# Seven-product feed-forwards: a third output bank, S4 in SBUF, additions to y ahead of the next S2 chain, slots in order of use, from the third group on

## What is computed

```
def swiglu(h, w_in, w_out):
    g, u = jnp.split(h @ w_in, 2, axis=-1)
    return (jax.nn.silu(g) * u) @ w_out
```

## Time and profile before

| | us |
|---|---|
| median of 3 runs | 3055.93 |
| lowest, highest | 3053.72, 3056.25 |
| profiled execution, its own time | 3053.14 |
| its span, first to last instruction | 3051.4 |
| TensorE busy in it | 2763.3 (91%) |
| VectorE busy | 1832.1 (60%) |
| GpSimd busy | 1509.9 (49%) |
| ScalarE busy | 1257.7 (41%) |
| mean granted clock of TensorE | 0.964 |

### The profile page before, as it was taken

One profiled execution on the slowest core, in us unless ns is written; L12 is line 12 of the kernel. 1 busy time (PEld: TensorE's weight loads), 2 busy tenths in 40 slices (PEclk: granted clock), 3 DMA queues, 4 the chain that ended last, 5 costly groups with the idle time before them and its releaser, 6 DMA issues. The chain is left out here.

```text
span 3051.4 us, 45625 instructions
## 1 busy us (share of the span) xinstructions
PE 2763.3 (91%) x17672; PEld 2453.7 (80%) x17672; DVE 1832.1 (60%) x3055; ACT 1257.7 (41%) x2315; POOL 1509.9 (49%) x982
## 2 busy tenths in 40 slices
PE   8989999999999999787889778889989999788888
PEld 6778888889998998677778677778877788677787
DVE  5787766776767784764566655565554423644444
ACT  3276432324453673333333333333455733333332
POOL 1333544445564333655664565565424444565563
PEclk7999999999999999898999899999999999999999
DMA  5324554435754222233343233343323222122221
GB/s 231 98 45 163 196 197 154 158 124 174 256 203 136 50 50 104 101 126 111 119 138 111 90 127 129 124 138 111 113 60 105 83 98 82 56 84 75 78 90 63
DMA packets 103923, 362.47 MB, mean 119 GB/s; under 512 B 12449, under 2 KB 14625, under 8 KB 102305
## 3 DMA queue, kind: packets, MB, share of 16 engines
q1 hardware_dynamic: 103714, 359.63, 35.1%
HBM read 338.61 MB, written 2.10 MB: 112 GB/s over the span
## 5 line engine op out<-in xcount | busy, mean ns | idle before, releaser
L333 POOL TENSOR_TENSOR w_lo<-raw,w_hi 128x1024 fp32r<-128x1024 f32 x259 | 655.9, 2538 | 680.7 <-ACT w_hi L327 623.3
L1159 POOL TENSOR_TENSOR w_lo<-raw,w_hi 128x512 fp32r<-128x512 f32 x261 | 347.7, 1336 | 301.2 <-ACT w_hi L1143 297.9
L327 ACT ACTIVATE w_hi<-raw 128x1024 fp32r<-128x1024 f32 x267 | 279.1, 1055 | 429.6 <-PE ps L356 387.2
L356 PE MATMUL ps<-ffn_hi,w_hi 128*128 128x512 f32 (+1 forms) x844 | 320.2, 379 | 136.9 <-DVE y L1452 92.9
L356 PE MATMUL ps<-h_hi,w_hi 128*128 128x512 f32 (+1 forms) x1096 | 363.2, 346 | 9.1 <-DVE h_lo L632 4.4
L356 PE MATMUL ps<-h_lo,w_hi 128*128 128x512 f32 (+1 forms) x1096 | 357.2, 341 | 0.0
L356 PE MATMUL ps<-h_hi,w_lo 128*128 128x512 f32 (+1 forms) x1096 | 357.1, 341 | 0.0
L356 PE MATMUL ps<-n_hi,w_hi 128*128 128x256 f32 (+1 forms) x880 | 304.8, 346 | 18.5 <-DVE n_lo L890 9.5
L356 PE MATMUL ps<-ffn_lo,w_hi 128*128 128x512 f32 (+1 forms) x844 | 313.2, 371 | 0.0
L356 PE MATMUL ps<-ffn_hi,w_lo 128*128 128x512 f32 (+1 forms) x844 | 311.9, 369 | 0.0
L356 PEld LDWEIGHTS ps<-ffn_hi,w_hi 128*128 128x128 f32 x844 | 167.3, 198 | 179.5 <-DVE y L1452 109.9
(11 more groups left out here) (393 smaller groups left out, 7369.7 us busy)
## 6 DMA issues: line engine op xcount, KB each, us to landing
raw<-w_stream SPq DMA_DIRECT2D x441, 512.0 KB, 3.4
modraw<-mod_stream SPq DMA_DIRECT2D x102, 512.0 KB, 5.2
mod_extra<-mod_stream SPq DMA_DIRECT2D x74, 512.0 KB, 5.3
mod_pair<-mod_first SPq DMA_DIRECT2D x7, 1024.0 KB, 12.5
l_qs<-l_q_hi SPq DMA_DIRECT2D x32, 128.0 KB, 2.3
l_qs<-l_q_lo SPq DMA_DIRECT2D x32, 128.0 KB, 2.3
l_qs<-l_q_hi SPq DMA_DIRECT2D x16, 192.0 KB, 2.9
l_qs<-l_q_lo SPq DMA_DIRECT2D x16, 192.0 KB, 3.5
```

The source lines that it names most:

```text
L327: nc.scalar.activation(w_hi[:, c % RING, :], raw[:, c % RING, :], ACT.Copy).then_inc(hi_ready, 1)
L333: nc.gpsimd.tensor_tensor(w_lo[:, c % RING, :], raw[:, c % RING, :], w_hi[:, c % RING, :].bitcast(F32), ALU.subtract).then_inc(lo_ready, 1)
L356: mm = nc.tensor.matmul(out, w[a], x[b][:, off:off + n], start=first and i == 0, stop=last and i == 2)
L1159: ins = nc.gpsimd.tensor_tensor(lo, item_raw(c, k), hi.bitcast(F32), ALU.subtract)
```

## The change

The last line of `ffn` gives all three feed-forwards banks 5, 6 and 2 for outputs, so that output n waits for the addition of output n-3. Bank 2 no longer holds S2; both chunks form S2 in bank 7, and S4 goes to a new SBUF buffer, `down_last`. The low parts of both S4 move from VectorE to GpSimd. The items take their slots, and GpSimd its low parts, in the order in which TensorE uses them, with outputs among them. Seven-product groups are groups 2 to 9; group 1 becomes direct. On VectorE the additions 0 to 2 stand ahead of S2 of the next group, addition 3 ahead of its low part and S4, addition 4 ahead of the second half of `seven_hidden` (now split off as `seven_third` and `seven_hidden`), S2 of b=1 moves to the start of the next group, `pair_u` goes ahead of bS2's low part, and mods part 1 goes from the end of the group to before addition 0. TensorE no longer starts outputs 0 and 1 with chunk 2g alone before it waits for chunk 2g+1. In group 0 both parts of the mods go ahead of the second hidden product and the input sums go behind the additions; their copies and low parts move to group 1. The core of the diff:

```
-                    outs=(5, 6, 2) if name == "l0_ffn" else (5, 6))
+                    outs=(5, 6) if name == "l0_ffnc" else (5, 6, 2))
...
-    POOL_LOWS = [A11, S3, S1, A12, A22] + [PARTS + k for k in (A11, S3, S1, A12, A22)] + [OUT_Q, OUT_Q + 1, OUT_Q + 2]
-    DVE_LOWS = [S2, S4, PARTS + S2, PARTS + S4]
+    POOL_LOWS = [A11, S3, S1, A12, PARTS + A11, A22, S4, PARTS + S3, PARTS + S1, PARTS + A12, OUT_Q, OUT_Q + 1, PARTS + A22,
+                 PARTS + S4, OUT_Q + 2]
+    DVE_LOWS = [S2, PARTS + S2]
...
-    SEVEN = NG - 2
+    SLOT_ORDER = PE_ORDER[:12] + [OUT_Q, OUT_Q + 1] + PE_ORDER[12:] + [OUT_Q + 2, OUT_Q + 3]
+    HI_ORDER = [A11, S2, S3, S1, A12, PARTS + A11, A22, S4, PARTS + S2, PARTS + S3, PARTS + S1, PARTS + A12, OUT_Q, OUT_Q + 1,
+                PARTS + A22, PARTS + S4, OUT_Q + 2, OUT_Q + 3]
+    FIRST_SEVEN, LAST_SEVEN = 2, NG - 2
+    SEVEN = LAST_SEVEN - FIRST_SEVEN + 1
...
     def turn_of(g, k):
 
-        return ITEMS * (g - 1) + k + min(max(g - 2, 0), 4)
+        i = SLOT_ORDER.index(k) if k < ITEMS else ITEMS
+        return 2 + ITEMS * (g - FIRST_SEVEN) + i + min(g - FIRST_SEVEN, 4)
...
-        for n in range(2):
-            bank_free(n)
-            out_part(n, 0)
         pe.wait_ge(hid_ready, CREDIT + f["m"] + 2 * g + 2)
-        for n in range(2):
-            out_part(n, 1).then_inc(out_ready, 1)
-        for n in range(2, 4):
+        for n in range(4):
             bank_free(n)
             out_part(n, 0)
             out_part(n, 1).then_inc(out_ready, 1)
...
     def seven_s4(dve, f, c, g, b):
-        dve.wait_ge(q_low_dve, before_items(f, g, 4) + 2 * b + 1)
-        y = down_bank(b)
-        nc.vector.tensor_tensor(y, raw_quarter(c + 2 * b, A12), y, ALU.subtract).then_inc(down_chain, 1)
+        i = chunks_done(f, g, b)
+        dve.wait_ge(q_low_dve, before_items(f, g, 2) + b + 1)
+        if i >= 1:
+            low_there(dve, f, c, g if b else g - 1, S4 if b else PARTS + S4)
+        nc.vector.tensor_tensor(down_last[:], raw_quarter(c + 2 * b, A12), down_bank(), ALU.subtract).then_inc(down_chain, 1)
...
+        seven_s2(dve, f, c, g, 1)
+        seven_u(dve, f, g, 0)
         item_low_dve(dve, f, c, g, PARTS + S2)
         seven_s4(dve, f, c, g, 1)
-        seven_u(dve, f, g, 0)
         seven_c22(dve, f, g, 0)
-        item_low_dve(dve, f, c, g, PARTS + S4)
         mods(0)
         seven_u(dve, f, g, 1)
+        seven_third(dve, f, g, 0)
         seven_hidden(dve, f, g, 0)
         ffn_hidden_lo(dve, f, 2 * g + 1, 0)
         seven_c22(dve, f, g, 1)
-        if g < SEVEN:
+        mods(1)
+        dve.wait_ge(out_free, f["free0"] + CREDIT + 8 * g)
+        for n in range(3):
+            add(n)
+        if g < LAST_SEVEN:
             seven_s2(dve, f, c + 6, g + 1, 0)
+        add(3)
+        if g < LAST_SEVEN:
             item_low_dve(dve, f, c + 6, g + 1, S2)
             seven_s4(dve, f, c + 6, g + 1, 0)
-        dve.wait_ge(out_free, f["free0"] + CREDIT + 8 * g)
-        for n in range(4):
-            add(n)
+        seven_third(dve, f, g, 1)
+        add(4)
         seven_hidden(dve, f, g, 1)
-        if g < SEVEN:
-            seven_s2(dve, f, c + 6, g + 1, 1)
-            item_low_dve(dve, f, c + 6, g + 1, S4)
-        for n in range(4, KC):
+        for n in range(5, KC):
             add(n)
         ffn_hidden_lo(dve, f, 2 * g + 2, 0)
-        mods(1)
...
         full_pool(pool, f, h, 0)
+        split_lo(pool, c0 + 4)
         full_pool(pool, f, h, 1)
-        split_lo(pool, c0 + 4)
+        split_lo(pool, c0 + 5)
+        split_lo(pool, c0 + 6)
         full_pool(pool, f, h, 2)
+        split_lo(pool, c0 + 7)
         full_pool(pool, f, h, 3)
...
+            if f["index"] > 0 and g == 0:
+                mods(g, 1, group)
             ffn_mult(dve, f, 2 * g + 2, 2 * gd, c + 2, d)
...
+            if f["index"] > 0 and g == 0:
+                in_sums_dve(dve, f)
+                return
             mods(g, 1, group)
```

More of the change, by code:

```diff
@@ L1065, in item_at @@
     def item_at(turn):
-        for g in range(1, SEVEN + 1):
-            if turn_of(g, 0) <= turn < turn_of(g, 0) + ITEMS:
-                return g, turn - turn_of(g, 0)
+        for g in range(FIRST_SEVEN, LAST_SEVEN + 1):
+            i = turn - turn_of(g, SLOT_ORDER[0])
+            if 0 <= i < ITEMS:
+                return g, SLOT_ORDER[i]
     def slot_views(f, turn):
@@ L1366, in seven_act @@
     def seven_act(act, f, c, g):
+        more = g < LAST_SEVEN
         def ahead(k):
[L1369 removed]
+            if more:
                 item_hi(act, f, c + 6, g + 1, k)
[L1372 to L1373 removed]
+        down_copy(act, f, g, 1)
         seven_first_copy(act, f, g, 0)
[L1375 removed]
+        for k in (PARTS + S2, PARTS + S3, PARTS + S1, PARTS + A12, OUT_Q, OUT_Q + 1):
             item_hi(act, f, c, g, k)
         seven_silu_first(act, f, g, 0)
[L1378 removed]
+        item_hi(act, f, c, g, PARTS + A22)
+        item_hi(act, f, c, g, PARTS + S4)
         seven_first_copy(act, f, g, 1)
[L1380 removed]
+        item_hi(act, f, c, g, OUT_Q + 2)
+        item_hi(act, f, c, g, OUT_Q + 3)
         seven_silu_second(act, f, g, 0)
[L1382 removed]
         ffn_hidden_hi(act, f, 2 * g + 1, 0, c, 0)
[L1384 to L1385 removed]
+        if more:
             ahead(A11)
@@ L1391, in seven_act @@
             prepare_last_act(act, f, c, 0)
+        seven_silu_first(act, f, g, 1)
+        if more:
+            ahead(A12)
+            ahead(PARTS + A11)
+        else:
             prepare_last_act(act, f, c, 1)
-        seven_silu_first(act, f, g, 1)
-        if g < SEVEN:
-            down_copy(act, f, g + 1, 1)
-            ahead(A12)
+        seven_silu_second(act, f, g, 1)
+        if more:
             ahead(A22)
+            ahead(S4)
         else:
             prepare_last_act(act, f, c, 2)
-        seven_silu_second(act, f, g, 1)
-        if g < SEVEN:
-            ahead(S4)
-            ahead(PARTS + A11)
         ffn_hidden_hi(act, f, 2 * g + 2, 0, c + 6, 0)
-        if g == SEVEN:
+        if not more:
             prepare_last_act(act, f, c, 3)
@@ L1506, in ffn_pool @@
         full_pool(pool, f, h, 0)
+        split_lo(pool, c0 + 4)
         full_pool(pool, f, h, 1)
-        split_lo(pool, c0 + 4)
+        split_lo(pool, c0 + 5)
+        split_lo(pool, c0 + 6)
         full_pool(pool, f, h, 2)
+        split_lo(pool, c0 + 7)
         full_pool(pool, f, h, 3)
-        for i in range(5, 8):
+        for i in range(8, 2 + 6 * FIRST_SEVEN):
             split_lo(pool, c0 + i)
-        for g in range(1, SEVEN + 1):
-            seven_pool(pool, f, c0 + 2 + 6 * g, g)
+        for g in range(FIRST_SEVEN, LAST_SEVEN + 1):
+            c = c0 + 2 + 6 * g
+            down_pool(pool, f, c, g, 0)
+            for k in (A11, S3, S1, A12, PARTS + A11):
+                item_low_pool(pool, f, c, g, k)
+            down_pool(pool, f, c, g, 1)
+            for k in POOL_LOWS[5:]:
+                item_low_pool(pool, f, c, g, k)
+            item_low_pool(pool, f, c, g, ITEMS - 1)
         for i in range(FFN_BLOCKS - RING, FFN_BLOCKS):
@@ L1848, in step @@
                 split_lo_dve(dve, c + 4)
+            if f["index"] > 0 and g == FIRST_SEVEN - 1:
+                mods(g, 0, group)
             ffn_mult(dve, f, 2 * g + 1, 2 * gd, c, d)
@@ L1852, in step @@
                 split_lo_dve(dve, c + 5)
-            if f["index"] > 0:
-                in_sums_dve(dve, f)
-            mods(g, 0, group)
-            if f["index"] > 0:
+            last_direct = f["index"] > 0 and g == FIRST_SEVEN - 1
+            if last_direct:
                 in_sums_low(dve, f)
-                seven_s2(dve, f, c + 6, 1, 0)
+                seven_s2(dve, f, c + 6, g + 1, 0)
+            else:
+                mods(g, 0, group)
+            if f["index"] > 0 and g == 0:
+                mods(g, 1, group)
             ffn_mult(dve, f, 2 * g + 2, 2 * gd, c + 2, d)
-            if f["index"] > 0:
-                item_low_dve(dve, f, c + 6, 1, S2)
-                seven_s4(dve, f, c + 6, 1, 0)
             if f["held"]:
```

102 lines of the change are left out of this document (43 added, 59 removed).

## The result

| | before | changed |
|---|---|---|
| median, us | 3054.82 | 2860.85 (4 runs, 2858.45 to 2864.26) |
| ratio to before, 95% interval | | 0.9366 [0.9349, 0.9382] |
| profiled execution, its own time; its span | 3053.14; 3051.4 | 2862.70; 2860.5 |
| GpSimd busy in it | 1509.9 (49%) | 1570.1 (55%) |
| mean granted clock | 0.964 | 0.981 |

The change takes 6.3% off the time: 194 us by the medians, 190.4 between the two profiled executions. The forecast was 2870. Where the time came from, by the stretches (columns as in the earlier trace rows: length, busy PE, PEld, DVE, ACT, POOL, PEclk, DMA, GB/s), in this order: groups 0 and 1 of F1, F2, F3; groups 2 to 9 of F1, F2, F3; one group of F1, one of F2, one of F3.

What follows compares the result with a forecast made beforehand. VectorE's order and the two output banks were taken to bind, not the work. Gains of 54.1, 11.3, 53.3 and 67.1 sum to 185.8 us off 3053.1: 2867.3, plus 2.8 for the median, 2870; range 2820 to 2930.

Steps and rivals of the forecast that it cites:

- Groups 0 and 1: First two groups of each feed-forward: group 0 from 122.7 to 68.6 us, group 1 from 118.1 to 106.8, in all three.
- Third bank and additions ahead, F3: Groups 2 to 9 of the third feed-forward: no output waits, 31.8 us a group, gain 53.3 us.
- Mods of part 1 before addition 0: Groups 2 to 9, first two feed-forwards: mod blocks land late, output n=3 waits 3.5 us; 36.5 us a group.
- The clock: Groups 2 to 9, first two feed-forwards: lower granted clock costs 1.3 us a group, bounds 0 and 3.5.
- The earlier slots from group 7 on: First two feed-forwards: slots come one item earlier from group 7, 35.2 us a group where earlier ones take 36.5.
- Group 2: First two feed-forwards: group 1's part 1 mods still stand ahead of group 2's pair_u, 2.5 us each, 5.0 together.
- GpSimd: Seven-product groups: GpSimd takes 25.8 us a group in the third feed-forward, 28 to 30 in the first two.
- Joining the halves of n=0 and n=1: Outputs 0 and 1: costs nothing while hidden chunk 2g+1 is there, 0.87 us of cover; without cover 1.4 us.
- the mod blocks in time: Rival, first two feed-forwards: only VectorE's own 5.3 us count, 33.6 us a group, total 2831; chance 0.20.
- The clock's rival: Rival, first two feed-forwards: blocks land at T+22, clock loses today's 8%, +2.5 us in 16 groups, 2910; chance 0.20.
- GpSimd as the bound: Rival, seven-product groups: 20 items at 2.25 us make 45 us a group, slower at 3114; chance 0.06.
- The bank does not help: Rival: additions wait behind something else on VectorE, groups 2 to 9 stay unchanged, total 2990; chance 0.04.

Runs made afterwards that it cites:

- experiment 1: Changed kernel with the third output bank undone for the seven-product feed-forwards (banks 5 and 6 only): 2912.0 us, ratio 0.9536.
- experiment 2: Changed kernel with the next group's S2, its low part and S4 again ahead of additions 0 to 3, three banks kept: 2922.2 us, ratio 0.9565.
- 3: Changed kernel with two output banks only and the next group's S2, low part and S4 ahead of the additions: 2970.5 us, ratio 0.9728.
- 4: Changed kernel with S2 of b=1 back ahead of additions 4 to 7 of the group before: 2924.0 us, ratio 0.9572.
- experiment 5: Changed kernel with third bank, order of the next group's S2 and S4, and place of S2 of b=1 all undone: 3017.9 us, ratio 0.9881.
- experiment 6: Changed kernel with three mod blocks loaded behind block c+5 and the fourth behind c+6: 2833.9 us, ratio 0.9276.
- 7: Changed kernel with the mods of part 1 moved from ahead of addition 0 to behind addition 4: 2815.0 us, ratio 0.9217.
- 10: Changed kernel with mods of part 1 behind addition 4 and part 0's first mod block loaded ahead of block c+5: 2799.0 us, ratio 0.9160.
- 12: The 2799.0 us kernel with group 1's second mod pair ahead of its addition 5, no longer ahead of group 2's pair_u: 2793.1 us, ratio 0.9137.
- Experiment 11: Changed kernel with group 0's second mod pair moved behind the additions' copies, ahead of the input sums: 2851.0 us, ratio 0.9334.
- experiment 9: Changed kernel with eight unused 256-column GpSimd additions in every seven-product group: 2874.9 us, ratio 0.9411.

## Why the prediction came out

The sum was 185.8 us off the profiled execution, measured are 190.4. The waits for additions went, and the one stop that was named is the one that is left, so the mechanism holds in F1 and F2; in F3 the result came as worked out, but mostly not from the parts named for it. That the total came so near is partly luck. Groups 0 and 1 gave 11.5 us less than forecast, groups 2 to 9 of F3 4.3 more and those of F1 and F2 13.5 more. By steps:

- *Third bank and additions ahead, F3.* 31.8 us a group forecast, 31.1 measured: no output waits, as worked out. But the credit was given to the wrong parts. Of the 8.0 us that groups 3 to 8 gained each, the bank and the order of the chain share 1.4 (experiments 1 to 3), S2 of b=1 is 3.1 when it is undone alone (4), and more than half lies outside the three (5: 39.1 before, 34.7 with them undone). The views of before could have shown this: the wait of 3.70 at n=6 is the larger of the two, and ahead of additions 4 and 5 stand the product of chunk 2g+2, 3.17 us idle for ScalarE, and S2 of b=1 (experiment 5).
- *Mods of part 1 before addition 0.* The step that I distrusted is the one stop left. Forecast: c+7 issued at T+14, block at T+19.3, addition 0 done at T+24.9, stop 3.5. Measured: T+14.1, T+18.8, T+24.1, stop 2.8. The term was 0.7 too large, as the block landed in 4.3 us; experiment 6 shows that the late block is 1.2 us of the stop, and 7 that the pair's place is all of it.
- *The clock.* 1.3 us a group were set down. F1 lost nothing in groups 3 to 9 (clock 1.00 in the row above), F2 some 1.2 a group (35.3 against 34.1 in groups 3 to 9). The forecast of 31.4 + 0.3 for the group without stops was 0.6 high; the prediction has 31.8 for the same group in F3 and does not say where 31.4 comes from. With these, 36.5 became 34.0 in F1 and 34 to 37 in F2. The earlier slots from group 7 on made no difference: 34.0 us in groups 3 to 6 of F1 and in 7 and 8.
- *Group 2.* 5.0 us for pair_u in F1 and F2; A12 stops 3.1 us in each, but the outputs of this group stop too (0.98 and 3.8 in F1) and the clock falls: 42.1 and 40.3 us against 34.1 and 35.3 for the groups after it, 13 us in place of 5. Experiments 10 and 12 take most of it away.
- *Groups 0 and 1.* The mis-sized term: a gain of 53.9 for 65.4. F3, without mods, came out at 54.5 for 55.6. F1 and F2 took 66.8 and 65.7 for 59.9; group 0 is 29.4 and 28.3 for 23.3, group 1 37.4 in both for 36.6. The mod product and its copy were priced from rows beside 512-column GpSimd instructions; group 0 has 1024-column ones. One pair was put at 5.3 us and is 7.1 (1651.31 to 1658.44), the second 8.9, and with both ahead of the copies TensorE stands for 3.6 at n=3. Experiment 11 gives 23.0 us for group 0 with the second pair behind; forecast 23.3.
- *GpSimd.* 25.8 us a group forecast for F3 and 28 to 30 for F1 and F2; 25.3 in groups 3 to 8 of F3 and 29.0 in F1. The S4 low parts cost nothing, as said.
- *Joining the halves of n=0 and n=1.* No stop at output 0 in F3 and in groups 3 to 9 of F1, one of 0.6 us in groups 3 to 9 of F2: next to nothing, as said.

What the mods cost follows one rule in the rows of F1 above, and the prediction misread it. VectorE's second product starts at 1431.64, when GpSimd's instruction has 0.99 us to go until 1432.63; 0.99 and its own 1.21 are 2.20, and it took 2.07. GpSimd's next starts at 1432.59, while the product runs until 1433.71; 1.12 and its own 1.29 are 2.41, and it took 2.24. The copy of two elements starts at 1433.76 and ends with that instruction. So each waits for what is left of the other's, and 1.21 + 1.29 is the most that a product can take, not what lock-out makes of every one. In the whole changed kernel 162 of the 172 mod products and copies that start beside a running GpSimd instruction took their own time and the rest of that instruction's, to 0.15 us. In group 0 the other party is 2.4 us long when alone, which gives the 3.36; the copy took 2.24 us there, against 0.17 in experiment 11 with GpSimd idle. The Trainium skill (SBUF — State Buffer, Who interferes with whom) calls the pair of ports that the two engines share an exclusive lock, and the one that comes second blocks. The rows agree with it, in group 0 and in the groups from 2 on. The same section of the Trainium skill says that a copy of VectorE can contend too, under conditions; the copy here does.

Of the rivals, the mod blocks in time (2831) is what experiment 6 built, at 2834. The clock's rival (2910) did not come; its two conditions, a block 1.3 us later and 2.2 us more for the clock, add up to 3.5 us a group and not to the 2.5 that it used. GpSimd as the bound fell by experiment 9. "The bank does not help" fell with the groups of 31.1 us, though in F3 the bank by itself is worth nothing (experiment 1).

## What to carry to other kernels

A queue of finished outputs is served by one engine in written order, so look at every instruction ahead of the next addition and ask for whom it waits; a difference that waits for another engine's sum, put ahead of an addition, cost more here (63 us) than a missing bank (51 us). When two such causes overlap, undoing one shows nothing in the stage where the other covers it: undo them singly and together. And price an instruction that shares a path with another engine as its own time and what can be left of the other's instruction, so by the size of what runs beside it.

## What the runs showed of the hardware

- A stop of 2.8 to 3.0 us, once in each group, cost no clock in groups 3 to 9 of F1 (1.00). The same groups of F2, with stops of 2.1 to 3.8 us, are at 0.97, with up to 21 matmuls of a group at the lower level; two of them have one of 2.8 us at n=3 and 7 and 10 such matmuls. In experiment 11 these groups of F2 had stops of 2.1 to 3.4 us and 1.00. So a loss of clock can't be read from a stop's length alone. What decides was not settled.
- A stop of 5.5 us at n=3 brought the lower level in each of groups 3 to 8 of F1 and F2 in experiment 2, the stop of 1.6 us in experiment 6 in none.
- VectorE's product with both inputs in SBUF and GpSimd's low part run one after the other, not together: whichever starts second is lengthened by what is left of the first (162 of 172 cases to 0.15 us). A copy of two elements does the same.
- Two products of 1.21 us and a copy of 0.17 us, work of 2.6 us, occupy VectorE for 4.65 us in the group of F1 above (GpSimd on 512 columns) and for 8.9 in group 0 (on 1024).
